# All 28 product tiles of a group added by VectorE, in a fused Strassen-type feed-forward loop on one core

## The chip, the core and the metric

The kernel runs on one core of one Trainium2 chip. TensorE (PE) multiplies, ScalarE (ACT), VectorE (DVE) and GpSimd (POOL) do the elementwise work, SyncE (SP) issues the transfers. The metric is the device time of one launch in microseconds (us). Before the change the median of three runs is 1248.9 us (1247.93 to 1248.97).

## The reference, cut to what matters

One layer of a hybrid encoder over 1088 kept rows (1024 of a prompt and 64 of a sample). The change touches only its second half, the feed-forward block:

```
f = square(relu(rmsnorm(h, norm_ffn_w) @ w_up)) @ w_down    # 1024 -> 4096 -> 1024, float32
h = h + f
y = rmsnorm(h)
```

## The kernel before, in words

A float32 product is made of three passes: each operand is split into a rounded high part (`_hi`, written by ScalarE with a Copy) and the rest (`_lo`, written by VectorE as source minus high part), and `passes` (L1419) issues high x high, high x low and low x high.

The 4096 hidden columns are worked through in 16 groups of 256. In each group TensorE first runs `up(g)`: two blocks of 128 hidden columns (a=0 and a=1), each in two halves of the inner dimension and three column ranges, 144 matmuls. ScalarE applies relu and square into `fr`. Then comes the down product. Groups 0 to 14 do it with seven products of 512x128x512 blocks in place of eight (a Strassen-Winograd scheme); the last group does it plainly. TensorE's order of products is P1, P2, P6, P5, P7, P4, P3. Each has four quarters q = 0 to 3 of three matmuls of 128x512, so 84 matmuls, and then `sample` adds 8 more. The operands of a product are one combination of `fr` blocks and one of `w_down` blocks:

```
P1: A11 x B11   P2: A12 x B21   P6: S2 x T2   P5: S1 x T1   P7: S3 x T3   P4: A22 x T4   P3: S4 x B22
```

S1 (sum) and S2 (difference) are built by VectorE (L1279, L1282), S3 and S4 by GpSimd, and T1, T3, T2, T4, in that order, by GpSimd from the loaded `w_down` blocks (L1386 to L1391). T4 is the last of a chain of dependent subtractions.

The products lie in eight PSUM banks: P1, P6, P7, P4 of a quarter share one bank (`BANK1`), P2, P5, P3 another (`BANK2`). P6, P7, P4 and P3 accumulate on what the bank holds, so between two products of a bank its content must have been taken: a quarter of P6 waits for the add of P1's same quarter, P5 for P2's, P7 for P6's, P4 for P7's, P3 for P5's. What is taken is added into `h` in SBUF. Before the change VectorE does this for 20 of the 28 quarter tiles (`add`, L1249). The 8 of P6 and P3 are copied by ScalarE from PSUM to one of four `tmp` tiles (`copy_out`, L796) and added to `h` by GpSimd (L1378); TensorE waits there for the copy (`act_copy`), not for the add.

The order on each engine is written out by hand in a function `group(g)` per engine, and each step waits for counting semaphores. Counters are read by position: `D_HI`, `D_LO`, `F_HI`, `F_LO` list in which order the high and low parts come, and a consumer waits for the position of its part. For P6 that is the low part of S2 (`f_ready`). The high part of `up`'s a=1 weights is written by ScalarE in `up_split(g, "up", 0)`, its low part by VectorE in `split_ffn(g, "up", 1, 0)`; TensorE's second block waits for that (`w_split`). SP's queue holds the loads only: four of `w_down` (`dr`) a group and four of `w_up` (`raw`).

Of the kernel before, what the change touches and what calls it, by code (L numbers as in the profile page):

```python
# [98 lines left out]
DVE_ADDS = [(P1, 0), (P1, 1), (P2, 0), (P1, 2), (P1, 3), (P2, 1), (P2, 2), (P2, 3), (P5, 0), (P5, 1), (P7, 0), (P7, 1),  # L99
            (P7, 2), (P7, 3), (P5, 2), (P5, 3), (P4, 3), (P4, 0), (P4, 1), (P4, 2)]  # L100
COPIES = [(P6, 0), (P6, 1), (P6, 2), (P6, 3), (P3, 0), (P3, 1), (P3, 2), (P3, 3)]
NPROD = 30
NDVE, NCOPY = len(DVE_ADDS), len(COPIES)
# [33 lines left out]
def build(nc, x_prompt, x_sample, state_conv, state_ret, meta_tokens, norm_mix_w, w_in, conv_w, ret_gn_w,  # L137
# [3 lines left out]
    with ctx:  # L141
# [45 lines left out]
        tmp2 = sb("tmp2", [P, 512], r_norm)  # L187
        tmp3 = sb("tmp3", [P, 512], r_norm + 2048)
# [114 lines left out]
        act_copy = sem("act_copy")  # L303
        pool_add = sem("pool_add")
# [67 lines left out]
        F_HI = ["f1", "A11", "S3", "A12", "f2", "A22", "S2", "S1", "f12", "S4"]  # L372
# [54 lines left out]
        def _(sp):  # L427
# [111 lines left out]
            sp.wait_ge(pool_add, NCOPY * G_LAST + 4)  # L539
# [15 lines left out]
        def _(act):  # L555
# [252 lines left out]
            def group(g):  # L808
                act.wait_ge(prod_done, NPROD * g + 1)
                up_split(g, "up", 0)  # L810
                d_hi(g, "B11")
                d_hi(g, "T1")
                d_hi(g, "B21")
                d_hi(g, "T3")
                act.wait_ge(f_ready, NF_PARTS * g + 1)
                relu(g, 0, 0)
                d_hi(g, "B22")
                square(g, 0, 0)
                relu(g, 0, 1)
# [20 lines left out]
                f_hi(g, "S1")  # L840
                copy_out(g, P6, 0)
                act.wait_ge(f_ready, NF_PARTS * g + F_LO.index("f1") + 2)
                act.activation(sf[:, 3, :], sf[:, 0, :].bitcast(F32), ACT.Copy, scale=-1.0).then_inc(neg_ready, 1)
                f_hi(g, "f12")
                copy_out(g, P6, 1)
                f_hi(g, "S4")
                copy_out(g, P6, 2)
                copy_out(g, P6, 3)
                copy_out(g, P3, 0)
                up_split(g, "next", 1)  # L850
                copy_out(g, P3, 1)
                copy_out(g, P3, 2)
                copy_out(g, P3, 3)
# [34 lines left out]
            def last_group(g):  # L888
# [3 lines left out]
                act.wait_ge(pool_add, NCOPY * g + 4)  # L892
# [36 lines left out]
        def _(dve):  # L929
# [27 lines left out]
            dve.sem_inc(pool_add, 4)  # L957
# [303 lines left out]
            def group(g):  # L1261
                split_ffn(g, "up", 1, 0)
                d_low(g, "B11", D_LO)
                split_ffn(g, "up", 1, 1)
                d_low(g, "T1", D_LO)
                d_low(g, "B21", D_LO)
                d_low(g, "B22", D_LO)
                f_low(g, "A11", F_HI)
                d_low(g, "T4", D_LO)
                f_low(g, "f1", F_HI)  # L1270
                split_ffn(g, "next", 0, 0)
                d_low(g, "T2", D_LO)
                f_low(g, "S3", F_HI)
                d_low(g, "T3", D_LO)
                f_low(g, "A12", F_HI)
                add(g, P1, 0)
                dve.wait_ge(fr_ready, 6 * g + 6)
                dve.tensor_tensor(f12[:, :], fr[:, 0, SEQ:TY], fr[:, 1, SEQ:TY], ALU.add).then_inc(f_sum_dve, 1)
                dve.tensor_tensor(fo_raw[:, P5, :], fr[:, 0, 512:1024], fr[:, 1, 512:1024], ALU.add).then_inc(f_sum_dve, 1)  # L1279
                dve.wait_ge(f_sum_dve, 3 * g + 2)  # L1280
                dve.wait_ge(f_sum_pool, 2 * g + 1)
                dve.tensor_tensor(fr[:, 0, 512:1024], fo_raw[:, P5, :], fr[:, 0, 0:512], ALU.subtract).then_inc(f_sum_dve, 1)  # L1282
                add(g, P1, 1)
                add(g, P2, 0)
                f_low(g, "S2", F_HI)
                add(g, P1, 2)
                add(g, P1, 3)
                f_low(g, "S1", F_HI)
                add(g, P2, 1)
                add(g, P2, 2)  # L1290
                add(g, P2, 3)
                add(g, P5, 0)
                f_low(g, "f2", F_HI)
                add(g, P5, 1)
                f_low(g, "A22", F_HI)
                add(g, P7, 0)
                add(g, P7, 1)
                add(g, P7, 2)
                add(g, P7, 3)
                f_low(g, "S4", F_HI)  # L1300
                add(g, P5, 2)
                add(g, P5, 3)
                f_low(g, "f12", F_HI)
                add(g, P4, 3)
                add(g, P4, 0)
                sample_add(g, 0)
                add(g, P4, 1)
                split_ffn(g, "next", 0, 1)
                add(g, P4, 2)
                sample_add(g, 1)  # L1310

# [60 lines left out]
        def _(pool):  # L1372
            def add(g, p, q):
                k = COPIES.index((p, q))
                pool.wait_ge(act_copy, NCOPY * g + k + 1)
                if p == P3:
                    pool.wait_ge(pool_add, NCOPY * g + n_copy(P6, q) + 4)
                pool.tensor_tensor(h_part(p, q), tmp(k), h_part(p, q), ALU.add).then_inc(pool_add, 1)  # L1378

            def group(g):  # L1380
# [14 lines left out]
                pool.wait_ge(f_sum_dve, 3 * g + 3)  # L1395
# [3 lines left out]
                add(g, P6, 2)  # L1399
                add(g, P6, 3)  # L1400
                add(g, P3, 0)
                add(g, P3, 1)
                add(g, P3, 2)
                add(g, P3, 3)
# [13 lines left out]
        def _(pe):  # L1418
# [212 lines left out]
            def up(g, first):  # L1631
                for a in range(2):
# [5 lines left out]
                    for half, j in order:  # L1638
# [24 lines left out]
            def product(g, p, q, first):  # L1663
# [19 lines left out]
                elif p == P7:  # L1683
                    pe.wait_ge(act_copy, NCOPY * g + n_copy(P6, q))
# [8 lines left out]
            def sample(g):  # L1693
# [74 lines left out]
```

## Time and profile before

| | before |
|---|---|
| median of 3 runs | 1248.9 us |
| the profiled execution's own time | 1246.07 us |
| its span | 1244.1 us |
| PE busy | 1226.6 us (99%), 6792 matmuls |
| DVE busy | 748.3 us (60%) |
| ACT busy | 500.5 us (40%) |
| POOL busy | 290.1 us (23%) |
| granted TensorE clock, mean | 0.997 |

The span is what the profile's clock covers; 1.97 us of the execution lie around it. A busy share is an average over the whole span. The feed-forward loop (groups 0 to 14) fills roughly the second half of it. A matmul's recorded duration overlaps with the next one's, so the pace is read from the difference of two starts.

### The profile page before, as it was taken

How to read it: one execution, taken by the hardware profiler on the slowest of the kernel's cores; microseconds unless marked ns; L12 is line 12 of the kernel's file. 1: busy time of each engine (PE TensorE's matmuls, PEld its weight loads, DVE VectorE, ACT ScalarE, POOL GpSimd, SP SyncE). 2: the span in 40 equal slices, each digit the busy share in tenths (PEclk: the TensorE clock that was granted, in tenths of full speed). 3: DMA queues.
4: the chain of work that ended last, by engine and by line, in shares of the span. 5: the costliest groups of instructions: out<-in, count | busy, mean ns of one | idle time of the engine just before them, and what ended most of it. 6: DMA issues, size and time to landing. Idle time of an engine off the chain costs nothing.

```text
span 1244.1 us, 20364 instructions
## 1 busy us (share of the span) xinstructions
PE 1226.6 (99%) x6792; PEld 1134.6 (91%) x6792; DVE 748.3 (60%) x1334; ACT 500.5 (40%) x1046; POOL 290.1 (23%) x221
## 2 busy tenths in 40 slices
PE   8999999999999999999999999999999999999997
PEld 5999999999999888889989989989988998998995
DVE  6555355355354554385686676677568667666747
ACT  6232232232232332255445335434544443543546
POOL 0000000000000000034533543352353354345212
PEclk9999999999999999999999999999999999999999
DMA  7111111111111530121012021021111202202103
GB/s 235 48 39 35 48 37 45 44 30 44 47 36 53 194 94 1 61 67 57 20 59 67 8 67 59 8 67 59 42 34 59 67 8 63 63 8 67 51 17 144
DMA packets 88353, 70.17 MB, mean 56 GB/s; under 512 B 9456, under 2 KB 73072, under 8 KB 88320
## 3 DMA queue, kind: packets, MB, share of 16 engines
q1 hardware_dynamic: 88320, 69.73, 18.3%
q8 instruction: 20, 0.33, 0.1%
q14 instruction: 13, 0.11, 0.0%
HBM read 64.73 MB, written 4.99 MB: 56 GB/s over the span
## 4 chain that ended last, share of the span: by engine, by line
PE 95%; DVE 2%; issue 1%; ACT 1%; DMA 1%; SPq 0%; POOLq 0%; POOL 0%; DVEq 0%; ACTq 0%
PE ps L1421 29%; PE ps L1423 29%; PE ps L1422 29%; PE ps L1427 1%; PE ps L1428 1%; PE ps L1599 1%; PE ps L1520 1%; PE ps L1538 1%; PE ps L1527 1%; PE ps L1537 1%; PE ps L1506 1%; PE ps L1438 0%; DMA raw<-in_w_up 0%; DVE hw L1338 0%; PE ps L1544 0%
## 5 line engine op out<-in xcount | busy, mean ns | idle before, releaser
L1421 PE MATMUL ps<-mid_hi,ws_hi 128*128 128x368 f32 (+1 forms) x768 | 251.3, 327 | 3.0 <-DVE ws_lo L1210 3.0
L1423 PE MATMUL ps<-mid_hi,ws_lo 128*128 128x368 f32 (+1 forms) x768 | 251.4, 327 | 0.0
L1422 PE MATMUL ps<-mid_lo,ws_hi 128*128 128x368 f32 (+1 forms) x768 | 250.7, 326 | 0.0
L1421 PE MATMUL ps<-hn_hi,ws_hi 128*128 128x368 f32 (+1 forms) x648 | 219.7, 339 | 1.2 <-DVE hn_lo L976 1.2
L1422 PE MATMUL ps<-hn_lo,ws_hi 128*128 128x368 f32 (+1 forms) x648 | 213.1, 329 | 0.0
L1423 PE MATMUL ps<-hn_hi,ws_lo 128*128 128x368 f32 (+1 forms) x648 | 213.0, 329 | 0.0
L1254 DVE TENSOR_TENSOR h<-ps,h 128x512 f32<-128x512 f32 x300 | 194.0, 679 | 9.1 <-PE ps L1423 9.1
L1378 POOL TENSOR_TENSOR h<-tmp,h 128x512 f32<-128x512 f32 x120 | 159.0, 1355 | 126.1 <-ACT tmp L799 126.1
L1421 PE MATMUL ps<-do_hi,fo_hi 128*128 128x512 f32 x452 | 176.3, 390 | 0.0
L1422 PE MATMUL ps<-do_lo,fo_hi 128*128 128x512 f32 x452 | 176.1, 390 | 0.0
L1423 PE MATMUL ps<-do_hi,fo_lo 128*128 128x512 f32 x452 | 176.0, 389 | 0.0
L1421 PEld LDWEIGHTS ps<-mid_hi,ws_hi 128*128 128x128 f32 x768 | 144.1, 188 | 4.2 <-DVE ws_lo L1210 3.3
L1210 DVE TENSOR_TENSOR ws_lo<-raw,ws_hi 128x512 fp32r<-128x512 f32 x64 | 60.5, 947 | 143.1 <-ACT ws_hi L753 143.1
L1422 PEld LDWEIGHTS ps<-mid_lo,ws_hi 128*128 128x128 f32 x768 | 144.2, 188 | 0.6
L1423 PEld LDWEIGHTS ps<-mid_hi,ws_lo 128*128 128x128 f32 x768 | 144.2, 188 | 0.0
L1386 POOL TENSOR_TENSOR do_raw<-dr 128x512 f32<-128x512 f32 x15 | 19.2, 1282 | 527.4 <-DMA dr<-in_w_down 526.8
L799 ACT ACTIVATE tmp<-ps 128x512 f32<-128x512 f32 x120 | 67.4, 597 | 151.1 <-PE ps L1423 151.1
L1421 PEld LDWEIGHTS ps<-hn_hi,ws_hi 128*128 128x128 f32 x648 | 121.8, 188 | 3.9 <-DVE hn_lo L976 2.4
L1422 PEld LDWEIGHTS ps<-hn_lo,ws_hi 128*128 128x128 f32 x648 | 121.9, 188 | 0.0
L1423 PEld LDWEIGHTS ps<-hn_hi,ws_lo 128*128 128x128 f32 x648 | 121.7, 188 | 0.0
L1421 PEld LDWEIGHTS ps<-do_hi,fo_hi 128*128 128x128 f32 x452 | 84.8, 188 | 18.5 <-DVE fo_lo L1247 0.3
L1423 PEld LDWEIGHTS ps<-do_hi,fo_lo 128*128 128x128 f32 x452 | 84.9, 188 | 18.0
(194 smaller groups left out, 1746.3 us busy)
## 6 DMA issues: line engine op xcount, KB each, us to landing
raw<-in_w_up SPq DMA_DIRECT2D x64, 256.0 KB, 4.8
dr<-in_w_down SPq DMA_DIRECT2D x64, 256.0 KB, 3.5
raw<-in_w_in SPq DMA_DIRECT2D x56, 256.0 KB, 2.9
raw<-in_w_out SPq DMA_DIRECT2D x16, 256.0 KB, 3.1
out<-hw SPq DMA_DIRECT2D x16, 256.0 KB, 2.1
xr<-in_x_prompt SPq DMA_DIRECT2D x7, 512.0 KB, 6.1
h<-in_x_prompt SPq DMA_DIRECT2D x2, 1024.0 KB, 10.8
h<-in_x_prompt SPq DMA_DIRECT2D x1, 2048.0 KB, 9.7
```

Of the source, the lines that this page charges most:

```text
L799: act.activation(tmp(k), bank_of(p, q)[:, :], ACT.Copy).then_inc(act_copy, 1)
L1210: dve.tensor_tensor(ws_lo[:, half], raw[:, s, :].rearrange("p (k c) -> p k c", k=4), ws_hi[:, half].bitcast(F32), ALU.subtract).then_inc(w ...
L1254: dve.tensor_tensor(h_part(p, q), bank_of(p, q)[:, :], h_part(p, q), ALU.add).then_inc(dve_add, 1)
L1378: pool.tensor_tensor(h_part(p, q), tmp(k), h_part(p, q), ALU.add).then_inc(pool_add, 1)
L1386: pool.tensor_tensor(t1, b12, b11, ALU.subtract).then_inc(d_sum, 1)
L1421: pe.matmul(out, a_hi, b_hi, start=start, stop=False, skip_group_check=again)
L1422: pe.matmul(out, a_hi, b_lo, start=False, stop=False, skip_group_check=again)
L1423: return pe.matmul(out, a_lo, b_hi, start=False, stop=stop, skip_group_check=again)
L1427: pe.matmul(out, a_hi_lo, b_hi, start=start, stop=False)
L1428: return pe.matmul(out, a_hi_lo, b_lo, start=False, stop=stop)
L1506: last = pe.transpose(out[:, c * P:(c + 1) * P], src[:, at:at + P], ident[:, :])
L1520: last = pe.matmul(out[:, c * HD:(c + 1) * HD], kd[:, c, :], v_tok[:, c0 + c, :], start=True, stop=True)
```

## The change

`COPIES`, the two semaphores and the four `tmp` steps of the middle go: no ScalarE copy out of PSUM and no GpSimd add in groups 0 to 14. VectorE's table has all 28 tiles, and every wait of TensorE on a copy becomes one on a VectorE add. The written orders of ScalarE and VectorE, and the four position lists, are new throughout.

```diff
-DVE_ADDS = [(P1, 0), (P1, 1), (P2, 0), (P1, 2), ... (P4, 1), (P4, 2)]
-COPIES = [(P6, 0), (P6, 1), (P6, 2), (P6, 3), (P3, 0), (P3, 1), (P3, 2), (P3, 3)]
+DVE_ADDS = [(P1, 0), (P1, 2), (P1, 1), (P1, 3), (P2, 0), (P2, 3), (P2, 2), (P6, 2), (P2, 1), (P6, 0), (P6, 1),
+            (P6, 3), (P7, 0), (P5, 1), (P7, 1), (P7, 3), (P7, 2), (P5, 0), ... (P3, 3), (P3, 1)]
-        F_LO = ["A11", "f1", "S3", "A12", "S2", "S1", "f2", "A22", "S4", "f12"]
+        F_LO = ["A11", "f1", "S3", "A12", "S1", "S2", "f2", "A22", "S4", "f12"]
-        D_HI = ["B11", "T1", "B21", "T3", "B22", "T2", "T4"]
-        D_LO = ["B11", "T1", "B21", "B22", "T4", "T2", "T3"]
+        D_HI = ["B11", "T4", "T3", "T1", "B22", "T2", "B21"]
+        D_LO = ["T4", "T3", "B22", "T2", "T1", "B11", "B21"]
...
             def group(g):                                   # ScalarE
                 act.wait_ge(prod_done, NPROD * g + 1)
+                d_hi(g, "B11")
+                d_hi(g, "T4")
+                d_hi(g, "T3")
                 up_split(g, "up", 0)
-                d_hi(g, "B11")
-                d_hi(g, "T1")
-                d_hi(g, "B21")
-                d_hi(g, "T3")
...
             def group(g):                                   # GpSimd
-                add(g, P6, 0)
-                add(g, P6, 1)
...
-                add(g, P3, 3)
...
                 elif p == P7:
-                    pe.wait_ge(act_copy, NCOPY * g + n_copy(P6, q))
+                    pe.wait_ge(dve_add, NDVE * g + n_dve_add(P6, q))
```

The negation of `f1` and the high part of the next group's second weight half also move forward on ScalarE, the small sum `f12` moves back on VectorE, and the load of the final norm weights no longer waits for GpSimd's adds, since the tiles that shared its place are gone.

Three places are shown as they stand in the engines' instruction orders. In the rows, `h<-ps` is an add of a tile, `fo_lo<-fr` the low part of A12 (first) or S2 (second), `fo_lo<-fo_raw` that of S1, `fo_raw<-fr` the sum S1, and `fr<-fo_raw,fr` the difference S2; ps0, ps1, ps2, ps6 are the banks of P1's quarters 0, 1, 2, 3.

VectorE at the first products of a group, before:

```order
L1254 TENSOR_TENSOR h_106<-ps0,h_106 128x512 [waits prod_done]
...
L1279 TENSOR_TENSOR fo_raw_55<-fr_61 128x512
...
L1282 TENSOR_TENSOR fr_61<-fo_raw_55,fr_61 128x512 [waits f_sum_pool]
...
L1254 TENSOR_TENSOR h_106<-ps1,h_106 128x512 [waits prod_done]
...
L1254 TENSOR_TENSOR h_106<-ps7,h_106 128x512 [waits dve_add]
...
L1247 TENSOR_TENSOR fo_lo_54<-fr_61,fo_hi_53 128x512 [waits f_hi_ready]
```

And the same place of the kernel after:

```order
L1229 TENSOR_TENSOR h_104<-ps0,h_104 128x512 [waits prod_done]
...
L1253 TENSOR_TENSOR fo_raw_55<-fr_61 128x512 [waits fr_ready]
...
L1229 TENSOR_TENSOR h_104<-ps2,h_104 128x512 [waits prod_done]
...
L1257 TENSOR_TENSOR fr_61<-fo_raw_55,fr_61 128x512 [waits f_sum_pool]
...
L1222 TENSOR_TENSOR fo_lo_54<-fo_raw_55,fo_hi_53 128x512 [waits f_hi_ready]
...
L1229 TENSOR_TENSOR h_104<-ps1,h_104 128x512 [waits prod_done]
...
L1229 TENSOR_TENSOR h_104<-ps6,h_104 128x512 [waits prod_done]
...
L1222 TENSOR_TENSOR fo_lo_54<-fr_61,fo_hi_53 128x512 [waits f_hi_ready]
```

The low part of S2 had two adds between it and the difference; it now has the low part of S1 and two adds, and one more add (P1's quarter 2) stands ahead of the difference.

VectorE a little later, after only: the adds of P2's quarters 3 and 2 (ps5, ps4), P6's quarter 2 (ps2), P2's quarter 1 (ps3) and P6's quarter 0 (ps0).

```order
L1229 TENSOR_TENSOR h_104<-ps5,h_104 128x512 [waits dve_add]
...
L1229 TENSOR_TENSOR h_104<-ps4,h_104 128x512 [waits dve_add]
L1225 REGISTER_ALU
L1229 TENSOR_TENSOR h_104<-ps2,h_104 128x512 [waits prod_done]
L1225 REGISTER_ALU
L1228 REGISTER_ALU [waits prod_done]
L1229 TENSOR_TENSOR h_104<-ps3,h_104 128x512 [waits dve_add]
L1225 REGISTER_ALU
L1229 TENSOR_TENSOR h_104<-ps0,h_104 128x512 [waits prod_done]
```

P2's quarter 1 is now taken behind P6's quarter 2; before, all of P2 was taken ahead of anything of P6.

ScalarE at a group's start, before, where `ws_hi` is the high part of the a=1 weights and `do_hi` that of a `w_down` block (from `dr`) or of a T (from `do_raw`):

```order
L753 ACTIVATE ws_hi_66<-raw_68 128x512 [waits raw_in0]
L771 REGISTER_ALU
L774 ACTIVATE do_hi_56<-dr_108 128x512 [waits dr_in0]
L773 ISA
L774 ACTIVATE do_hi_56<-do_raw_58 128x512 [waits d_sum]
```

And after:

```order
L764 ACTIVATE do_hi_56<-dr_106 128x512 [waits dr_in0]
L763 ISA
L764 ACTIVATE do_hi_56<-do_raw_58 128x512 [waits d_sum]
L763 REGISTER_ALU
L764 ACTIVATE do_hi_56<-do_raw_58 128x512 [waits d_sum]
L787 ISA
L742 REGISTER_ALU [waits w_used]
L743 ACTIVATE ws_hi_66<-raw_68 128x512 [waits raw_in0]
```

The high part of the weights stood first and now stands behind those of T4 and T3.

## Rows read from the trace of the kernel before

**Rows 1.** The page: busy share, and the costliest rows of lines (engine, shape, count | busy, mean ns | idle before)

```profile
PE 1226.6 (99%) x6792; PEld 1134.6 (91%) x6792; DVE 748.3 (60%) x1334; ACT 500.5 (40%) x1046; POOL 290.1 (23%) x221
...
L1421 PE MATMUL ps<-mid_hi,ws_hi 128*128 128x368 f32 (+1 forms) x768 | 251.3, 327 | 3.0 <-DVE ws_lo L1210 3.0
...
L1254 DVE TENSOR_TENSOR h<-ps,h 128x512 f32<-128x512 f32 x300 | 194.0, 679 | 9.1 <-PE ps L1423 9.1
L1378 POOL TENSOR_TENSOR h<-tmp,h 128x512 f32<-128x512 f32 x120 | 159.0, 1355 | 126.1 <-ACT tmp L799 126.1
```

**Rows 2.** Busy by stretch: stretch, us, PE, PEld, DVE, ACT, POOL, PEclk, DMA, GB/s

```profile
854.64:899.29 44.65, 44.65 (x238) 40.97 (x237) 30.40 (x46) 20.24 (x42) 18.67 (x14) 1.00 0.15 47
...
654.00:698.60 44.60, 44.60 (x238) 40.96 (x237) 30.41 (x47) 20.25 (x42) 18.66 (x15) 1.00 0.16 47
```

**Rows 3.** Timeline, PE, one group's first products: start, duration, what

```profile
899.29 0.40 PE L1421 MATMUL ps<-do_hi,fo_hi 128*128 128x512 f32 x1
...
899.76 0.39 PE L1423 MATMUL ps<-do_hi,fo_lo 128*128 128x512 f32 x1
...
901.12 0.39 PE L1423 MATMUL ps<-do_hi,fo_lo 128*128 128x512 f32 x1
...
904.75 0.39 PE L1421 MATMUL ps<-do_hi,fo_hi 128*128 128x512 f32 x1
```

**Rows 4.** Timeline, DVE, the same group

```profile
900.18 0.69 DVE L1254 TENSOR_TENSOR h<-ps,h 128x512 f32<-128x512 f32 x1 [0.18 <-PE ps L1423]
...
903.61 0.76 DVE L1247 TENSOR_TENSOR fo_lo<-fr,fo_hi 128x512 fp32r<-128x512 f32 x1
...
908.98 1.32 DVE L1243 TENSOR_TENSOR sf<-fr,sf 128x64 fp32r<-128x64 f32 x1
...
910.82 1.21 DVE L1247 TENSOR_TENSOR fo_lo<-fr,fo_hi 128x512 fp32r<-128x512 f32 x1
911.95 2.47 DVE L1254 TENSOR_TENSOR h<-ps,h 128x512 f32<-128x512 f32 x4
914.34 0.68 DVE L1247 TENSOR_TENSOR fo_lo<-fo_raw,fo_hi 128x512 fp32r<-128x512 f32 x1
```

**Rows 5.** Timeline, ACT, the same group

```profile
899.99 0.50 ACT L784 ACTIVATE fr<-fr 128x352 f32<-128x352 f32 x1
```

**Rows 6.** Timeline, POOL, the same group and the four T of the group's start

```profile
878.24 1.28 POOL L1386 TENSOR_TENSOR do_raw<-dr 128x512 f32<-128x512 f32 x1
...
882.10 1.29 POOL L1391 TENSOR_TENSOR do_raw<-dr,do_raw 128x512 f32<-128x512 f32 x1
...
902.51 1.30 POOL L1396 TENSOR_TENSOR fo_raw<-fr 128x512 f32<-128x512 f32 x1 [10.82 <-DVE fr L1282]
906.40 5.08 POOL L1378 TENSOR_TENSOR h<-tmp,h 128x512 f32<-128x512 f32 x4 [2.58 <-ACT tmp L799]
```

**Rows 7.** Timeline, group 0: PE, ACT, DVE and POOL

```profile
527.06 0.32 PE L1423 MATMUL ps<-mid_hi,ws_lo 128*128 128x352 f32 x1
530.37 0.43 PE L1421 MATMUL ps<-mid_hi,ws_hi 128*128 128x368 f32 x1 [2.98 <-DVE ws_lo L1210]
530.64 0.33 PE L1422 MATMUL ps<-mid_lo,ws_hi 128*128 128x368 f32 x1
...
528.50 0.61 ACT L774 ACTIVATE do_hi<-dr 128x512 fp32r<-128x512 f32 x1
529.02 0.61 ACT L774 ACTIVATE do_hi<-do_raw 128x512 fp32r<-128x512 f32 x1
...
528.62 1.69 DVE L1210 TENSOR_TENSOR ws_lo<-raw,ws_hi 128x512 fp32r<-128x512 f32 x1 [5.37 <-ACT ws_hi L753]
...
527.27 1.26 POOL L1386 TENSOR_TENSOR do_raw<-dr 128x512 f32<-128x512 f32 x1 [526.82 <-DMA dr<-in_w_down]
```

**Rows 8.** Busy by stretch, the span's start and group 0 (columns as in rows 2)

```profile
10.20:14.00 3.80, 3.80 (x10) 1.72 (x9) 3.73 (x6) 3.31 (x7) 0.00 (x0) 0.56 1.13 342
527.00:530.40 3.40, 0.41 (x4) 0.12 (x2) 1.78 (x2) 2.44 (x5) 3.13 (x3) 1.00 0.81 231
```

More of the change, by code:

```diff
@@ L835, in group @@
                 relu(g, 1, 2)
+                act.wait_ge(f_ready, NF_PARTS * g + F_LO.index("f1") + 2)
+                act.activation(sf[:, 3, :], sf[:, 0, :].bitcast(F32), ACT.Copy, scale=-1.0).then_inc(neg_ready, 1)
                 square(g, 1, 2)
+                up_split(g, "next", 1)
                 f_hi(g, "f2")
                 f_hi(g, "A22")
+                f_hi(g, "S1")
                 f_hi(g, "S2")
[L840 to L843, printed above, removed]
                 f_hi(g, "f12")
-                copy_out(g, P6, 1)
                 f_hi(g, "S4")
[L847 to L853, printed above, removed]
             with act.Fori(0, G_LAST) as g:
@@ L1261, in group @@
             def group(g):
+                d_low(g, "T4", D_LO)
                 split_ffn(g, "up", 1, 0)
-                d_low(g, "B11", D_LO)
+                d_low(g, "T3", D_LO)
                 split_ffn(g, "up", 1, 1)
-                d_low(g, "T1", D_LO)
-                d_low(g, "B21", D_LO)
+                f_low(g, "A11", F_HI)
+                f_low(g, "f1", F_HI)
                 d_low(g, "B22", D_LO)
[L1268 to L1271, printed above, removed]
                 d_low(g, "T2", D_LO)
                 f_low(g, "S3", F_HI)
-                d_low(g, "T3", D_LO)
+                d_low(g, "T1", D_LO)
+                d_low(g, "B11", D_LO)
+                d_low(g, "B21", D_LO)
+                split_ffn(g, "next", 0, 0)
                 f_low(g, "A12", F_HI)
@@ L1277, in group @@
                 dve.wait_ge(fr_ready, 6 * g + 6)
-                dve.tensor_tensor(f12[:, :], fr[:, 0, SEQ:TY], fr[:, 1, SEQ:TY], ALU.add).then_inc(f_sum_dve, 1)
                 dve.tensor_tensor(fo_raw[:, P5, :], fr[:, 0, 512:1024], fr[:, 1, 512:1024], ALU.add).then_inc(f_sum_dve, 1)
-                dve.wait_ge(f_sum_dve, 3 * g + 2)
+                add(g, P1, 2)
+                dve.wait_ge(f_sum_dve, 3 * g + 1)
                 dve.wait_ge(f_sum_pool, 2 * g + 1)
                 dve.tensor_tensor(fr[:, 0, 512:1024], fo_raw[:, P5, :], fr[:, 0, 0:512], ALU.subtract).then_inc(f_sum_dve, 1)
+                f_low(g, "S1", F_HI)
                 add(g, P1, 1)
+                add(g, P1, 3)
+                f_low(g, "S2", F_HI)
                 add(g, P2, 0)
[L1285 to L1288, printed above, removed]
+                f_low(g, "f2", F_HI)
+                add(g, P2, 3)
+                add(g, P2, 2)
+                add(g, P6, 2)
                 add(g, P2, 1)
-                add(g, P2, 2)
-                add(g, P2, 3)
-                add(g, P5, 0)
[L1293 to L1300, printed above, removed]
+                add(g, P6, 0)
+                f_low(g, "A22", F_HI)
+                add(g, P6, 1)
+                add(g, P6, 3)
+                dve.tensor_tensor(f12[:, :], fr[:, 0, SEQ:TY], fr[:, 1, SEQ:TY], ALU.add).then_inc(f_sum_dve, 1)
+                add(g, P7, 0)
+                add(g, P5, 1)
+                add(g, P7, 1)
+                add(g, P7, 3)
+                add(g, P7, 2)
+                f_low(g, "S4", F_HI)
+                add(g, P5, 0)
                 add(g, P5, 2)
                 add(g, P5, 3)
+                add(g, P3, 0)
                 f_low(g, "f12", F_HI)
@@ L1305, in group @@
                 add(g, P4, 0)
+                split_ffn(g, "next", 0, 1)
+                add(g, P3, 2)
+                add(g, P4, 1)
                 sample_add(g, 0)
-                add(g, P4, 1)
-                split_ffn(g, "next", 0, 1)
                 add(g, P4, 2)
+                add(g, P3, 3)
                 sample_add(g, 1)
+                add(g, P3, 1)
             with dve.Fori(0, G_LAST) as g:
@@ L1372, in _ @@
         def _(pool):
[L1373 to L1378, printed above, removed]
             def group(g):
```

56 lines of the change are left out of this document (19 added, 37 removed).

## The prediction, made before the changed kernel ran

> **What bounds the kernel now.** I read the page first: PE is busy 99% of the span, DVE 60%, ACT 40%, POOL 23% [rows 1]. Then the busy table by stretch, one group each: a group takes 44.60 to 44.65 us and PE is busy for all of it, at granted clock 1.00 [rows 2]. The list of waits has no PE wait inside groups 1 to 14. The only one of the feed-forward part is in group 0, 2.98 us, where PE waits for VectorE's low part of the second weights [rows 1, 7]. So PE sets the time, and nothing that ACT, DVE or POOL are spared can be won back, except 2.98 us in group 0 and what the pace of matmuls varies: the two stretches differ by 0.05, which over 15 groups is 0.75 us. The question is therefore not how much work goes, but whether every wait of PE still ends ahead of it under the new orders.
>
> **Whether VectorE has the capacity.** A group now has 8 more adds. Four adds in a row and the next start are 914.34 - 911.95 = 2.39 apart, so an add takes 0.60 of the queue, though it is recorded as 0.68 [rows 4]. That adds 8 x 0.60 = 4.8 us. Some comes back. The 64-column low part takes 1.32 us at 908.98 while POOL adds (906.40, four of 1.27 each), and the low part of A22 takes 1.21 in place of 0.68 [rows 4, 6]. Both have two operands in SBUF and wait for POOL's instruction to end; the PSUM adds beside them don't. Without POOL's adds some 1.1 + 0.5 = 1.6 us return. The Trainium skill says the same ("SBUF — State Buffer", section "Who interferes with whom": VectorE with two SBUF inputs and a GpSimd instruction that reads SBUF lock each other out for a whole instruction), and by that rule alone the change would be free, which is the first rival below. VectorE goes from 30.40 to about 30.4 + 4.8 - 1.6 = 33.6 of 44.65 [rows 2]. As a mean it has room. The 120 ScalarE copies and 120 GpSimd adds that go [rows 1] were hidden under PE: worth 0.
>
> **Term 1, the low part of S2 in each of 15 groups.** I walk VectorE's new queue beside PE of the profiled group. P1's first matmul starts at 899.29, P6's at 904.75, 24 matmuls later, so a matmul takes p = 0.2275 [rows 3]. From the third matmul of a quarter (899.76) to its add (900.18) are 0.42 [rows 3, 4].
> - add of P1 quarter 0: 900.18, as before.
> - sum S1: 900.78. The last square of `fr` ends at 900.49 [rows 5]; the negation, now ahead of it, makes that less than 0.1 later, still in time.
> - add of P1 quarter 2: its third matmul is at 901.12 [rows 3], so 901.54. This is a new wait.
> - difference S2: 902.14. It ends at 902.83.
> - low part of S1: 902.74. ScalarE's queue up to its high part is square, weights, f2, A22, S1, about 900.49 + 0.5 + 0.15 + 0.5 + 0.6 = 902.3, in time. The high part of S2 follows the difference and is there at 903.5.
> - adds of P1 quarters 1 and 3: 903.34 and 903.94.
> - low part of S2: 904.54, ends 0.69 later at 905.23. POOL's S4 (1.30 long [rows 6]) starts when the low part of S1 lets go, about 903.4, and can add up to 0.1.
>
> Before, that low part ran from 903.61 to 904.37 [rows 4], 0.38 ahead of PE at 904.75. Now PE is 0.48 early. What a restart costs is in group 0: DVE ends at 528.62 + 1.69 = 530.31, PE starts at 530.37 (0.06), and its first matmul is recorded as 0.43 against 0.33 of the next ones, since its weights weren't loaded ahead (0.10) [rows 7]. So this stall is 0.48 + 0.16 = 0.64 us. Bounds: 0 if the adds ran closer than 0.60 apart (four would have to save 0.12 each), 0.75 with POOL's lock.
>
> **Term 2, two waits that the new add order makes.** (a) P5 quarter 1 waits for the add of P2 quarter 1, which now stands behind that of P6 quarter 2. Counted from P6's first matmul, P6's quarter 2 issues its last at 8p = 1.82, its add starts at +0.42, P2's at +0.60 and ends at +0.69: 3.53. PE wants P5 quarter 1 at 15p = 3.41. Late by 0.12, with the restart 0.28. (b) P4 quarter 2 waits for the add of P7 quarter 2, which stands behind that of quarter 3. From P7's first matmul: 11p + 0.42 + 0.60 + 0.69 = 4.21 against 18p = 4.10, late by 0.11, with the restart 0.27. In both VectorE is free when the product ends, so they don't hang on its load. Each lies between 0.1 (the weights of the waiting matmul load in the shadow of the one before) and 0.3; near zero if the adds come 0.1 sooner. I take 0.23 each, 0.46 together. Everything else that waits for an add (P7 for P6, P3 for P5, both blocks of `up` for P4 and P3, `sample`) comes out 0.3 us or more ahead; closest is P3's first quarter, behind P5's add and the low part of S4.
>
> Terms 1 and 2 are 0.64 + 0.46 = 1.1 us a group, and 15 groups 16.5 us. PE has no slack in which to catch up.
>
> **Term 3, group 0.** ScalarE now does the high parts of B11, T4 and T3 ahead of that of the a=1 weights. In groups 1 to 14 this is hidden: POOL no longer ends its adds at 878.2 and starts the four T when the last product ends, and PE needs the weights 12 us into the group. In group 0 there is no such lead: the `w_down` blocks land at 527.27 (the releaser of POOL's first T), when PE has just finished the first block (527.06) [rows 7]. Undisturbed, the four T take 882.10 + 1.29 - 878.24 = 5.15 [rows 6], so T4 is there at 532.42. High part of T4 532.5; that of T3 0.52 later (529.02 - 528.50 [rows 7]), 533.0; the weights 533.5 to 534.2; VectorE's low part to 534.9; PE at about 534.95. Before, 530.37 [rows 7]. That is 4.6 us, once. Bounds: 4.0 (ScalarE's queue pitch less) and 5.8 (VectorE in between, as in POOL's slower chain).
>
> PE is then idle for 7.6 us, from the end of its last matmul (527.06 + 0.32) to 534.95. An idle of 2.98 left the clock at 1.00 [rows 8]. At the span's start, after waits of a few us with few matmuls, the rows show a stretch at 0.56 of full speed, that is at the 1.2 GHz level nearly throughout 3.8 us [rows 8]: at half pace it loses 0.44 x 3.8 = 1.7 us. I add that 1.7 once; bounds 0 and twice that. The Trainium skill ("TensorE: Matmul & The Clock Gate", section "What's actually happening") has the engine fall to half clock after idleness; the rows at the start agree, and no row here shows it after an idle as long as this one.
>
> **Terms at nothing.** The load of the final norm weights starts earlier than it did; its first user comes over 20 us later. The rest of the ScalarE and VectorE reordering hides behind `up`, where both are often idle. The last group's order is unchanged except for one wait that is over by then.
>
> **Sum.** 16.5 + 4.6 + 1.7 = 22.8 us over the profiled execution: 1246.07 + 22.8 = 1268.9. The median shown is 2.8 above that execution, so on its scale 1248.9 + 22.8 = 1271.7; I predict 1271. Low end: half of terms 1 and 2 (8.3) with 4.0 is 1261. High end: 15 x 1.4 + 5.8 + 3.4 = 30.2, so 1279.
>
> **Rivals.**
> - *The freed lock wins; not slower.* VectorE gets 1.6 us a group back [rows 4, 6], and every new order ends in time. Place: the low part of S2 at 904.54; it decides if the queue ahead of it is 0.5 us shorter, and T4 must come by 528. For it: POOL's adds and ScalarE's copies are gone and PE alone was the bound. Against: the time is returned later than the place (from 908.98 on), and ahead of S2 no row shows a lock to lift. Price: -0.75 at best, 1248. Chance 7% (faster by over 0.2% 3%, within it 4%; 0.2%, 2.5 us, is what a measurement of this kernel can tell from no change).
> - *Only group 0.* Terms 1 and 2 are too large by 0.5 and 0.1 us each, and PE's waits end in time; 4.6 + 1.7 remain: 1255. For it: the margins are below 0.5 us. Against: two of the three follow from fixed durations. Chance 9%.
> - *VectorE becomes the bound in the products.* From P1's first add on it has 28 + 2 adds, S1, S2, four low parts and one of weights, 37 x 0.60 = 22.2 us, beside 92 matmuls x 0.2275 = 20.9 of PE, and only the tail in `up` takes the rest. If an add beside busy PE costs its recorded 0.68, 28 x 0.08 = 2.2 more a group come on top less some 1 us of margin: 15 x 1.2 = 18, so 1289. Against: rows 4 show 0.60. Chance 9%.
> - *The forecast*, 1261 to 1279: 75%.
>
> The range that I give is 1257 to 1281. Faster 0.03, same 0.04, slower 0.93.
>
> **What would show it.** In the profile after: PE idle before lines of P6's first matmul, by the low part of S2, about 0.5 to 0.6 us in each of 15 groups; two more of 0.1 to 0.3 by VectorE's adds; in group 0 an idle of 7.6 in place of 2.98, by the low part of the weights, and after it a stretch at half clock; a group of 45.7 in place of 44.6; VectorE's 64-column low part back at 0.2. The forecast is wrong if a group stays at 44.7, if the waits of PE name something else (a copy of the weights, S4, `sample`), or if group 0 alone differs.

## The result, and the profile after

The changed kernel takes **1275.25 us** (median of four runs, 1272.81 to 1276.42), the kernel before 1248.66 in the same comparison (1247.93 to 1248.97). The ratio is 1.0214, with a 95% interval of 1.0201 to 1.0228. The change costs 26.6 us, 2.1%. The profiled execution of the changed kernel took 1272.81 us, its span is 1271.0. Against the profiled execution before (1246.07) that is 26.7 more, where the forecast had 22.8.

The page of the changed kernel: busy time by engine, and the rows of part 5 that answer to [rows 1].

```profile
PE 1240.2 (98%) x6792; PEld 1132.4 (89%) x6792; DVE 777.6 (61%) x1454; ACT 438.4 (34%) x926; POOL 131.7 (10%) x101
...
L1229 DVE TENSOR_TENSOR h<-ps,h 128x512 f32<-128x512 f32 x420 | 272.5, 685 | 25.5 <-PE ps L1391 21.6
L1389 PE MATMUL ps<-mid_hi,ws_hi 128*128 128x368 f32 (+1 forms) x768 | 252.4, 329 | 7.8 <-DVE ws_lo L1185 7.8
...
L1389 PE MATMUL ps<-do_hi,fo_hi 128*128 128x512 f32 x452 | 181.7, 402 | 8.9 <-DVE fo_lo L1222 8.3
```

ScalarE lost 62 us of work and GpSimd 158, VectorE gained 29, and PE, which does the same 6792 matmuls, now waits. The list of waits of PE gives the same two by line, time, count and longest:

```profile
PE ps L1389 <- DVE fo_lo L1222: 8.3, 15, 0.6
PE ps L1389 <- DVE ws_lo L1185: 7.8, 1, 7.8
```

Fifteen waits of 0.55 for the low part of S2, and one of 7.8 in group 0. These two sums understate the first: a start of PE can be late with no idle written beside it. So I read the starts. In full flow they are 0.2275 apart [rows 3]. Three places of each group stand out, here in the profiled group (PE, start and duration first):

```profile
875.24 0.39 PE L1391 MATMUL ps<-do_hi,fo_lo 128*128 128x512 f32 x1
876.18 0.49 PE L1389 MATMUL ps<-do_hi,fo_hi 128*128 128x512 f32 x1 [0.55 <-DVE fo_lo L1222]
876.51 0.39 PE L1390 MATMUL ps<-do_lo,fo_hi 128*128 128x512 f32 x1
...
879.49 0.39 PE L1391 MATMUL ps<-do_hi,fo_lo 128*128 128x512 f32 x1
879.90 0.50 PE L1389 MATMUL ps<-do_hi,fo_hi 128*128 128x512 f32 x1
...
885.95 0.39 PE L1391 MATMUL ps<-do_hi,fo_lo 128*128 128x512 f32 x1
886.36 0.50 PE L1389 MATMUL ps<-do_hi,fo_hi 128*128 128x512 f32 x1
...
922.28 0.49 PE L1389 MATMUL ps<-do_hi,fo_hi 128*128 128x512 f32 x1 [0.55 <-DVE fo_lo L1222]
```

- P6's first matmul (876.18) starts 0.94 after the one before it, and the next start is 0.33 later, since its weights weren't loaded ahead: 0.94 + 0.33 - 2 x 0.2275 = 0.82 us lost.
- P5's quarter 1 (879.90) and P4's quarter 2 (886.36): 0.41 and then 0.34 (the next starts are at 880.24 and 886.70), so 0.30 each. No idle is written beside them. That the weights come late here too stands in PE's weight loads: in full flow a load starts some 0.2 ahead of its matmul, here with it.
- The same place of the next group is at 922.28, 46.10 later, where a group took 44.65 [rows 2]. The three places make 1.42 of the 1.45.

```profile
879.90 0.19 PEld L1389 LDWEIGHTS ps<-do_hi,fo_hi 128*128 128x128 f32 x1 [0.44 <-DVE h L1229]
```

The busy table of this stretch (columns as in [rows 2]) has VectorE at 32.4, forecast 33.6, and a PE that is no longer busy throughout:

```profile
876.18:922.28 46.10, 45.51 (x237) 40.77 (x237) 32.44 (x55) 16.13 (x34) 8.17 (x6) 1.00 0.15 46
```

VectorE in that group, from P1's first add on. P1's first matmul is at 870.01, where [rows 3] have 899.29:

```profile
870.90 0.69 DVE L1229 TENSOR_TENSOR h<-ps,h 128x512 f32<-128x512 f32 x1 [0.18 <-PE ps L1391]
871.51 0.68 DVE L1253 TENSOR_TENSOR fo_raw<-fr 128x512 f32<-128x512 f32 x1
872.26 0.69 DVE L1229 TENSOR_TENSOR h<-ps,h 128x512 f32<-128x512 f32 x1
872.87 0.68 DVE L1257 TENSOR_TENSOR fr<-fo_raw,fr 128x512 f32<-128x512 f32 x1
873.47 0.69 DVE L1222 TENSOR_TENSOR fo_lo<-fo_raw,fo_hi 128x512 fp32r<-128x512 f32 x1
874.07 1.28 DVE L1229 TENSOR_TENSOR h<-ps,h 128x512 f32<-128x512 f32 x2
875.27 0.68 DVE L1222 TENSOR_TENSOR fo_lo<-fr,fo_hi 128x512 fp32r<-128x512 f32 x1
875.87 0.69 DVE L1229 TENSOR_TENSOR h<-ps,h 128x512 f32<-128x512 f32 x1
876.47 0.22 DVE L1218 TENSOR_TENSOR sf<-fr,sf 128x64 fp32r<-128x64 f32 x1
```

The low part of S2 starts 5.26 after P1's first matmul; the forecast's walk had 904.54 - 899.29 = 5.25. It ends at 875.95, and PE starts 0.23 later. The 64-column low part takes 0.22 in place of the 1.32 of [rows 4].

Group 0, timelines of ScalarE, VectorE and PE (against [rows 7]), then the busy table by stretch, with the clock after the column of POOL:

```profile
531.47 1.15 ACT L764 ACTIVATE do_hi<-do_raw 128x512 fp32r<-128x512 f32 x2 [8.27 <-POOL do_raw L1367]
532.52 0.61 ACT L743 ACTIVATE ws_hi<-raw 128x512 fp32r<-128x512 f32 x1
533.17 0.69 DVE L1185 TENSOR_TENSOR ws_lo<-raw,ws_hi 128x512 fp32r<-128x512 f32 x1 [0.35 <-ACT ws_hi L743]
533.91 0.68 PE L1389 MATMUL ps<-mid_hi,ws_hi 128*128 128x368 f32 x1 [7.84 <-DVE ws_lo L1185]
534.38 0.51 PE L1390 MATMUL ps<-mid_lo,ws_hi 128*128 128x368 f32 x1
```

```profile
527.20:533.90 6.70, 0.00 (x0) 0.00 (x0) 1.43 (x3) 2.44 (x6) 4.15 (x4) 0.74 0.14 39
533.90:540.00 6.10, 6.08 (x27) 6.09 (x28) 3.78 (x6) 4.24 (x10) 1.41 (x1) 0.72 0.00 0
540.00:547.00 7.00, 7.00 (x45) 7.00 (x44) 3.35 (x6) 3.91 (x8) 0.00 (x0) 1.00 0.04 14
```

PE is idle 7.84 in place of 2.98, and the clock falls during that idle. After it the matmuls start about 0.31 apart until 537.14 instead of 0.17. Forty steps from the restart on take 8.23 us, and 6.71 in the kernel before: 1.5 us. The other three runs of the changed kernel have a mean granted clock of 0.992 to 0.994 where the profiled one has 0.996, and are 1.5 to 3.6 us longer.

The account of the profiled execution goes by PE's starts. The first matmul of the down product is at 547.39 in group 0 and at 1238.87 in group 15, before at 542.33 and 1211.71: 691.5 us against 669.4, so 22.1 in the loop, or 1.47 a group. Group 0 adds 7.84 - 2.98 = 4.9 of idle and 1.5 of half clock. It loses 1.3 because the work ahead of the idle happened to run that much faster in this execution (PE's last matmul before it starts at 525.75 against 527.06 in [rows 7]). Together 27.2; the spans differ by 26.9, the times by 26.7.

### The profile page after: what moved, and what is told of

Its sections match the earlier page's. It is cut to its first block, busy times and chain, and to the rows that moved or that the text cites. A ratio compares the mean times of both kernels' runs of the same rounds, so it can differ in the third digit from the quotient of the medians.

```text
span 1271.0 us, 20003 instructions
## 1 busy us (share of the span) xinstructions
PE 1240.2 (98%) x6792; PEld 1132.4 (89%) x6792; DVE 777.6 (61%) x1454; ACT 438.4 (34%) x926; POOL 131.7 (10%) x101
## 4 chain that ended last, share of the span: by engine, by line
PE 90%; DVE 5%; issue 2%; DMA 1%; ACT 1%; DVEq 0%; POOL 0%; SPq 0%; POOLq 0%; ACTq 0%
PE ps L1389 28%; PE ps L1391 27%; PE ps L1390 27%; DVE fo_lo L1222 2%; PE ps L1396 1%; PE ps L1395 1%; DVE h L1229 1%; PE ps L1567 1%; PE ps L1488 1%; PE ps L1506 1%; PE ps L1495 1%; PE ps L1505 1%; PE ps L1474 1%; DMA xr<-in_x_prompt 0%; DVE hn_lo L951 0%
## 5 line engine op out<-in xcount | busy, mean ns | idle before, releaser
L1229 DVE TENSOR_TENSOR h<-ps,h 128x512 f32<-128x512 f32 x420 | 272.5, 685 | 25.5 <-PE ps L1391 21.6
L1389 PE MATMUL ps<-do_hi,fo_hi 128*128 128x512 f32 x452 | 181.7, 402 | 8.9 <-DVE fo_lo L1222 8.3
L1390 PEld LDWEIGHTS ps<-do_lo,fo_hi 128*128 128x128 f32 x452 | 85.0, 188 | 15.9
L925 DVE TENSOR_TENSOR ws_lo<-raw,ws_hi 128x512 fp32r<-128x512 f32 x54 | 37.1, 689 | 88.6 <-ACT ws_hi L555 88.1
L1185 DVE TENSOR_TENSOR ws_lo<-raw,ws_hi 128x512 fp32r<-128x512 f32 x64 | 44.0, 689 | 70.3 <-ACT ws_hi L743 70.3
```

Source lines behind the costliest of these rows:

```text
L925: dve.tensor_tensor(ws_lo[:, s], raw[:, s, :].rearrange("p (k c) -> p k c", k=4), ws_hi[:, s].bitcast(F32), ALU.subtract).then_inc(w_split, 1)
L1185: dve.tensor_tensor(ws_lo[:, half], raw[:, s, :].rearrange("p (k c) -> p k c", k=4), ws_hi[:, half].bitcast(F32), ALU.subtract).then_inc(w ...
L1229: dve.tensor_tensor(h_part(p, q), bank_of(p, q)[:, :], h_part(p, q), ALU.add).then_inc(dve_add, 1)
L1389: pe.matmul(out, a_hi, b_hi, start=start, stop=False, skip_group_check=again)
L1390: pe.matmul(out, a_hi, b_lo, start=False, stop=False, skip_group_check=again)
```

## The experiments

Theory: three orders cost the time, each at the place that the forecast names (S2's part behind the S1 and P1 adds; two pairs of adds turned round; the a=1 weights behind T4 and T3). Main rival: 28 adds are simply too many for VectorE beside the products, whatever their order. Ratios are to the kernel before, run beside each.

**The a=1 weights first.** The changed kernel with one order undone:

```
# ScalarE, VectorE, start of a group
+up_split(g, "up", 0)   /  +split_ffn(g, "up", 1, 0)
 d_hi B11, T4, T3       /   d_low T4
-up_split(g, "up", 0)   /  -split_ffn(g, "up", 1, 0)
```

> The changed kernel with one thing undone: at a group's start ScalarE and VectorE split the a=1 weights ahead of T4 and T3 again. Theory (term 3 of the prediction): T4's chain held these weights up in group 0 alone. PE's idle there falls from 7.84 to about 3 us (weights landing only), the stretch at half clock after it goes with it, and a group of the loop stays at 46.1 us: 4.9 + 1.5 to 3.5 us less, 1267 to 1269. Rival (the second half of the weights or B11 is late next, since VectorE now sits before T4 instead): the idle in group 0 only moves to a later wait of the same group, and less than 3 us are won.

Measured 1268.99 us, ratio 1.0164 (1.0147 to 1.0181). PE's wait in group 0:

```profile
530.95 0.44 PE L1389 MATMUL ps<-mid_hi,ws_hi 128*128 128x368 f32 x1 [3.33 <-DVE ws_lo L1185]
```

The idle falls from 7.84 to 3.33 and the loop keeps its period (P6's first matmul at 873.27 and 919.41, 46.14). So the order of the weights made these 4.5 us of idle; the median is 6.3 lower. The median is at the upper end of the theory's range, but a part of the theory missed, for the half clock did not go with the long idle: from 531.77 to 535.15 matmuls still start up to 0.31 apart, though the profiled kernel before shows no half clock after 2.98.

**S1 and S2 as before.** The orders of the two sums' parts as before the change, the adds of P1 in quarter order; the rest as changed.

```
-F_HI = [.., "S1", "S2", ..]   DVE_ADDS = [(P1,0),(P1,2),(P1,1),(P1,3),..
+F_HI = [.., "S2", "S1", ..]   DVE_ADDS = [(P1,0),(P1,1),(P1,2),(P1,3),..
-S1, P1.2, S2, low S1, P1.1, P1.3, low S2
+S1, S2, P1.1, P1.2, low S2, P1.3, low S1
```

> The changed kernel, with the sum S1, the difference S2 and its low part back at the places in VectorE's queue that they had before the change (no add of P1's quarter 2 ahead of the difference, low part of S2 ahead of that of S1). Theory A (the three waits of a group are separate prices): the 0.82 us at P6's first matmul go, 15 x 0.82 = 12.3 us less, 1263. Theory B (VectorE's queue between P1 and P5 is full, and a wait taken away ahead comes back behind): P6 starts 0.8 us earlier but P2's quarter 1 is added only about 0.5 us earlier, so the wait at P5's quarter 1 grows from 0.29 to about 0.6, and a group falls from 46.1 to 45.6: 7.5 us less, 1268.

Measured 1265.96 us, ratio 1.0137 (1.0120 to 1.0153). PE at P5's quarter 1 and VectorE ahead of it:

```profile
878.07 0.39 PE L1391 MATMUL ps<-do_hi,fo_lo 128*128 128x512 f32 x1
878.76 0.50 PE L1389 MATMUL ps<-do_hi,fo_hi 128*128 128x512 f32 x1 [0.30 <-DVE h L1229]
879.10 0.40 PE L1390 MATMUL ps<-do_lo,fo_hi 128*128 128x512 f32 x1
```

```profile
873.57 0.81 DVE L1222 TENSOR_TENSOR fo_lo<-fr,fo_hi 128x512 fp32r<-128x512 f32 x1
874.30 0.68 DVE L1229 TENSOR_TENSOR h<-ps,h 128x512 f32<-128x512 f32 x1
...
876.10 0.21 DVE L1218 TENSOR_TENSOR sf<-fr,sf 128x64 fp32r<-128x64 f32 x1
876.24 3.07 DVE L1229 TENSOR_TENSOR h<-ps,h 128x512 f32<-128x512 f32 x5
```

P6 no longer waits, but the wait at P5's quarter 1 grows from 0.30 to 0.69 + 0.34 - 0.455 = 0.58. A group is 45.50 (878.76 to 924.26): of 0.82 only 0.60 came back. From 874.30 to the end of the five adds VectorE's starts stand 0.60 apart (0.13 behind the small one) without a pause. PE's wait at P6 had given this queue time, and without it the queue is late at the next place. The terms are not separable, as theory B had it; the measured median lies between the two theories.

**The turned adds put in order.** P2.1 ahead of P6.2, and P7.2 ahead of P7.3:

```
-P2.0, P2.3, P2.2, P6.2, P2.1   ..   P7.1, P7.3, P7.2
+P2.0, P2.3, P2.2, P2.1, P6.2   ..   P7.1, P7.2, P7.3
```

> The changed kernel with two swaps in VectorE's order: the add of P2's quarter 1 ahead of that of P6's quarter 2, and that of P7's quarter 2 ahead of that of quarter 3. Theory (term 2): both small waits come from an add queued behind one whose product has only just ended; they go whole, 0.59 us a group, 15 x 0.59 = 8.9 less, 1266, and PE's first matmul of P6 still waits 0.55 with a restart of 0.23 + 0.10. Rival (VectorE is simply full, so that the order of adds doesn't matter): the waits turn up at other quarters and a group stays above 45.9, within 3 us of 1275.

Measured 1265.41 us, ratio 1.0137 (1.0120 to 1.0154). Both small waits are gone, P6's stays, and a group is 45.46 (873.99 to 919.45). Taken off: 9.8 us of the median, 0.64 a group in the trace.

**Which wait stands first in PE's queue.** PE starts P6 0.23 after the low part's end. Behind the wait for that part its queue holds two more, for `d` and for the bank. Here the late one comes last:

```
-wait f_ready; wait d_ready; wait dve_add
+wait dve_add; wait d_ready; wait f_ready
```

> The changed kernel with nothing moved but the order of PE's own waits ahead of a product's first quarter: f_ready (the operand's low part) is waited for last, behind d_ready and dve_add. In the trace PE starts 0.23 us after the low part of S2 ends, but 0.05 us after an add that it waits for at a later quarter. Theory C (the waits behind the late one are still to be processed by PE's sequencer once it is released): the start falls to 0.05 to 0.1 us behind, 0.13 to 0.18 a group, 2 to 2.7 us less in all, 1272.5 to 1273. Rival (the 0.23 belongs to the low part as a written operand, or to its weights' load): no change, a group stays at 46.1.

Measured 1273.04 us, ratio 1.0192 (1.0175 to 1.0209).

```profile
877.76 0.39 PE L1391 MATMUL ps<-do_hi,fo_lo 128*128 128x512 f32 x1
878.53 0.50 PE L1389 MATMUL ps<-do_hi,fo_hi 128*128 128x512 f32 x1 [0.38 <-DVE fo_lo L1222]
```

```profile
877.80 0.68 DVE L1222 TENSOR_TENSOR fo_lo<-fr,fo_hi 128x512 fp32r<-128x512 f32 x1
```

PE now starts 0.05 after the part ends (878.48), as it does after an add, and the gap is 0.77 in place of 0.94. A group is 45.93 (878.53 to 924.46), 0.17 less. So the waits that stand behind a late one in the queue cost 0.17 to 0.18 us each time, although they are over. The trace shows this, the times alone don't: the median is 2.2 lower, as the theory had it, but the two intervals of the ratio overlap.

**All three orders mended, and the loop's two alone.** The first has the three edits above (the weights, S1 and S2, the turned adds), with all adds of P2 and P6 in quarter order and P5's quarter 0 taken ahead of P7's. The second leaves the a=1 weights behind T4 and T3.

> All 28 adds stay on VectorE, and all three causes are undone together: the weights' split first at a group's start, S1 and S2 in VectorE's queue as before the change, and the adds of P1, P2, P6 and P7 in the order of their quarters (P5's quarter 0 ahead of P7's). Theory (the loss is order alone, VectorE has room for 28 adds): no wait of PE in groups 1 to 14, a group of 44.6 to 44.7 us, an idle of about 3.3 in group 0, and 1248 to 1250, that is the time of the kernel before, within 1.5 us. Rival (VectorE is the bound of the products, so that some wait stays whatever the order): a group of 45.0 or more, 1254 or more.

> As the kernel with all three undone, but the weights of group 0 still stand behind T4 and T3. Theory: the loop is free of waits (44.6 to 44.7 a group) and what is left is group 0 alone: 4.9 us of idle more and 1.5 to 3.5 us of half clock behind it, 1254 to 1257. Rival (the idle in group 0 pushes the products of group 0 or later ones out of step, or the loop gives nothing back without it): over 1259.

Measured 1250.77 (ratio 1.0022, 1.0013 to 1.0030) and 1255.10 (1.0049, 1.0035 to 1.0062). 24 of the 26.6 us are gone, so the orders made them, though the first stays 0.8 above its theory's range. In both a group is 44.83 (871.89 to 916.72 in the first), 0.18 over [rows 2], one wait at P4's quarter 1. The first kernel's VectorE there:

```profile
869.70 0.21 DVE L1273 TENSOR_TENSOR f<-fr 128x64 f32<-128x64 f32 x1
869.83 3.20 DVE L1229 TENSOR_TENSOR h<-ps,h 128x512 f32<-128x512 f32 x5
```

Five adds take 3.20 here, 3.07 in the run of S1 and S2 above. P5.1 and P7.1 stand side by side here and add into the same part of `h`, so the kernel makes the second wait by a semaphore for the end of the first. It starts 0.72 after it (870.43 and 871.15), where others start 0.60 apart. The second kernel, idle 8.39 in group 0, differs from the first by 4.3 us.

**All three, and the loads of `w_up` first.** In group 0 `w_down`'s blocks are asked for ahead of `w_up`'s. The edit, on the kernel with all three orders mended and on the kernel before itself:

```
-load_down(0, True)
 group(0, False)
+load_down(0, True)
```

> The kernel with all three undone, and in SP's queue the four w_up loads of group 0 ahead of its four w_down loads, which wait for the last transposition. Theory: the only wait left in the feed-forward part is for the landing of these weights; they come earlier, the idle of about 3 us goes and with it any stretch at half clock, 1245 to 1246, faster than both kernels by 3 us. Rival (the splits of these weights wait for PE to be done with the first block anyway, so the earlier landing is hidden): under 1 us less than without it.

> The kernel before the change with only the swap of loads in group 0. Theory (where the adds are done is worth nothing once nothing waits for them; only the load order is worth 3 us): the same 1245 as the kernel with 28 VectorE adds and this swap, within 1 us. Rival (VectorE freed from waiting on GpSimd's adds is worth something in the end): 1 us or more above that kernel.

Measured 1248.97 (ratio 1.0005, 0.9997 to 1.0014) and 1243.57 (0.9958, 0.9946 to 0.9971). Both theories missed: the first kernel won under 2 us by the swap, and the two are 5.4 apart where they were to be the same. PE's wait in the second block of `up` of group 0, first in the kernel with all three, then in the kernel before with swapped loads:

```profile
535.72 0.44 PE L1389 MATMUL ps<-mid_hi,ws_hi 128*128 128x368 f32 x1 [2.35 <-DVE ws_lo L1185]
...
536.16 0.47 PE L1391 MATMUL ps<-mid_hi,ws_lo 128*128 128x368 f32 x1
536.43 0.51 PE L1389 MATMUL ps<-mid_hi,ws_hi 128*128 128x368 f32 x1
```

```profile
534.74 0.43 PE L1421 MATMUL ps<-mid_hi,ws_hi 128*128 128x368 f32 x1 [0.98 <-DVE ws_lo L1210]
```

With the swap the wait moves from the first half of the a=1 weights to the second. What holds it for 2.35 in the first kernel is ScalarE, which still has T4 and T3 ahead of it (the row of two):

```profile
532.14 1.15 ACT L764 ACTIVATE do_hi<-do_raw 128x512 fp32r<-128x512 f32 x2 [5.33 <-POOL do_raw L1367]
...
534.32 0.62 ACT L743 ACTIVATE ws_hi<-raw 128x512 fp32r<-128x512 f32 x1
```

The kernel before won 4.6 us by the swap. Its two traces show 2.0 of that, 0.98 of idle for 2.98. The other runs with the loads as they were have a mean granted clock of 0.993 to 0.997, those with the swap 0.997 to 0.998, which fits a stretch at half clock in most of the former; no trace of one was kept.

**28 adds with every order as before.** This separates the route of the adds from the orders: no copies, no adds on GpSimd, but the parts of `d` and of the weights too in the order of the kernel before, and P5.1 ahead of P7.0. Once with the loads as they were, once swapped.

```
 D_HI, D_LO, F_HI, F_LO and both queues up to P1.0: as in the kernel before
-P5.0, P7.0, P5.1, P7.1     (of the kernel with all three mended)
+P5.0, P5.1, P7.0, P7.1
```

> All 28 adds on VectorE from PSUM and no copies, as in the changed kernel, but every order as in the kernel before: the d parts and the weight splits on ScalarE and VectorE, S2 ahead of S1, the adds in quarter order, and P5 q1's add two places behind P5 q0 and ahead of P7 q0's, so that no two adds into the same part of h stand side by side. Theory (the 28 adds cost nothing by themselves, only the orders did; the 0.18 us left per group with all three orders mended was the dependent pair of adds): group 44.65, no start of PE beyond 0.30 us in the loop, group 0 as before with 2.98 of idle; time 1247 to 1249, the same as before. Rival 1 (the eight further adds leave VectorE too full somewhere whatever the order): a wait of 0.2 to 0.6 us per group stays, group 44.8 to 45.3, time 1250.5 to 1258. Rival 2 (the GpSimd adds held VectorE up and their absence helps): below 1247.

> The same kernel, and the loads of w_up for group 0 issued ahead of those of w_down. If the two changes are independent it takes off what the load swap took off the kernel before, 4.6 us: 1243 to 1244.5 beside 1243.6 for the kernel before with the swapped loads, no half-clock stretch in group 0, and one wait of about 1 us for the second half of the a=1 weights. If the half-clock stretch after a 2.35 us idle comes back as in the run with all three mended and the loads swapped: 1246 to 1248.

Measured 1249.36 (ratio 1.0014, 1.0005 to 1.0023) and 1245.82 (0.9988, 0.9979 to 0.9997). The theory gave 1247 to 1249 and 1243 to 1244.5, so both missed, by 0.4 and 1.3 us. The rival of a wait whatever the order comes nearest. A group is 44.77, 0.12 over [rows 2], nearly the same in both. In the first kernel's group 0 the idle was 3.66, not 2.98, and a stretch at half clock followed (starts 0.31 apart from 532.30 to 535.36 in its trace), which the theory did not have either. The first kernel's VectorE and then PE:

```profile
870.42 0.21 DVE L1273 TENSOR_TENSOR f<-fr 128x64 f32<-128x64 f32 x1
870.55 3.07 DVE L1229 TENSOR_TENSOR h<-ps,h 128x512 f32<-128x512 f32 x5
```

```profile
871.88 0.50 PE L1389 MATMUL ps<-do_hi,fo_hi 128*128 128x512 f32 x1
872.22 0.39 PE L1390 MATMUL ps<-do_lo,fo_hi 128*128 128x512 f32 x1
```

P7.0 is the second of the five: 871.15 to 871.83, and P4's first matmul starts 0.05 later. Here the rival has a small part of the truth: the queue is full at this place, and a sum of 64 columns that nobody needs yet, at 870.42, takes 0.13 of it.

**That sum one place behind P7.0.** The last kernel, loads swapped:

```
-add P5.0; f12; add P5.1; add P7.0; add P7.1
+add P5.0; add P5.1; add P7.0; f12; add P7.1
```

> The kernel with the old orders and the loads swapped, with the 64-column sum f12 on VectorE one place behind P7 q0's add instead of two places ahead of it. In the run without this edit the queue is full from 864.36 on, f12 takes 0.13 us of it, and PE starts P4's first matmul at 867.62, 0.04 us after P7 q0's add ends, with 0.12 us lost per group (group 44.77). Theory (what is left of the change's cost is just this place of a full queue): the add ends 0.13 us earlier, the wait goes, group 44.65 to 44.68, 1.5 to 1.9 us in 15 groups: 1243.5 to 1244.8. Rival (the wait moves behind, to P4 q1 and P7 q1's add, as the other mended waits did): group 44.75 to 44.80, time 1245 to 1246.5.

Measured **1244.61** us (1243.68 to 1244.97), ratio 0.9973 (0.9963 to 0.9982). The time is in the theory's range, the group just above it: 44.70 (the second matmul of P4's quarter 1 at 823.24 and 867.94), with that matmul still 0.05 late. From group 0 to group 15 the first matmuls of the down product are 670.6 us apart (540.32 and 1210.95), in the kernel before with the same loads 669.5 (540.78 and 1210.31). So with the adds all from PSUM and the orders right, the change still costs 0.07 a group. The kernel beats both kernels by the loads, not by the change: the kernel before with the same loads stands at 0.9958.

## Why the prediction was right, and where it was off

The time, the sign and the three places came out as forecast (1271 against 1275.25). The sizes were too small together: in the profiled execution 22.1 + 4.9 + 1.5 = 28.5, forecast 22.8. That the total there is only 26.7 owes 1.3 us to luck, the faster work ahead of group 0. By its steps:

- **VectorE's walk** was exact: 5.25 forecast, 5.26 measured, each step 0.60 apart as read from [rows 4], so the rival in which adds cost their recorded 0.68 was wrong. The queue went to 32.4 of 46.1, not to the bound.
- **Term 1**, 0.64 a group forecast, 0.82 measured. The lateness was right; the restart was 0.16 from [rows 7], measured 0.23 + 0.10. In group 0 the waiting matmul has no further waits behind the late one, at P6 it has two. Reversing their order gave the 0.17 back.
- **Term 2**, 0.46 forecast, 0.59 measured. Its working gave 0.28 and 0.27, each measured 0.30. The step that failed is the choice of 0.23, taken because weights might load in the shadow. They don't: the load starts with the matmul (879.90), and the next start comes 0.34 later, as at the other wait. Putting the adds in order removed both.
- **Term 3**, 4.6 forecast, 4.9 measured; weights first took the idle to 3.33. The half clock came, 1.5 in the profiled execution against 1.7, and by the other runs' clocks more than that in them. This is the likely reason why the median is 2.4 above the profiled execution; the traces with S1 and S2 as before and with the order of PE's waits show such a longer stretch, to 542.10 and 542.23.
- **Terms at nothing**: the copies and the GpSimd adds were worth nothing. The last three kernels without them never beat the kernel with them, at equal loads.
- **The freed lock** returned what it should (0.22 for 1.32), behind the place that was late. The Trainium skill ("SBUF — State Buffer", section "Who interferes with whom") says that a VectorE instruction with two SBUF inputs contends with a GpSimd one that reads SBUF, and one with at most one SBUF input, outside the two-port modes, doesn't. The trace agrees: with S1 and S2 as before the low part of S2 beside GpSimd's sum S4 (872.53 to 873.83) takes 0.81 in place of 0.68, and the PSUM adds keep 0.60. That lock comes from S4 and not from the adds that went, so ahead of the place that was late the change gave nothing back.
- **Not in the forecast**: the terms can't be taken off one by one. The S2 order alone was worth 0.60 of its 0.82 a group, because the queue behind it was full. The forecast's own sum of 37 x 0.60 = 22.2 against 20.9 said this, and I used it only for a rival.

What stays open is the size of a rest of 1 to 2 us between the kernel with 28 adds and the kernel before, both with swapped loads. The medians differ by 1.0; the traces show 1.1 in the loop and 0.18 of wait in group 0 (1.16 against 0.98). The ratios, each against its own runs of the kernel before, differ by 0.0015, which is 1.9 us, with intervals of 0.0010 and 0.0013 to each side.

## What to carry to other kernels

Where one engine is busy all the time, work taken from the others is worth nothing, and every instruction that a reordering puts ahead of something that this engine needs can cost. Walk the feeding queue from the last fixed event with the pitch of its starts, not with recorded durations, and check each consumer's time against it, one by one. Mend all the late places together, because a wait that goes uncovers the next, and put the wait that comes last at the end of the list.

## What the runs showed of the hardware

- **A start after a wait.** PE starts 0.05 after its releaser ends when no wait stands behind the late one (878.48 to 878.53), 0.23 when two do (875.95 to 876.18). The weights of that matmul add 0.10 to 0.11 at each of these waits.
- **Dependent adds.** Two adds on VectorE of which the second waits by a semaphore for the end of the first start 0.72 apart (870.43 and 871.15), others 0.60.
- **The clock after short idles.** An idle of 2.98 [rows 7] left the clock at 1.00 in the profiled execution, and so did 0.98, 1.14 and 1.16 with the loads swapped. After 2.35, 3.33, 3.35 and 3.66 it fell to the 1.2 GHz level for some 3 us, the first longer step beginning 0.4 to 1.0 us after the restart. In the five runs with idles of 7.84 to 8.65 it fell during the idle. Two of them by stretch, first the kernel with weights first, then that with all three and swapped loads (idle 2.35; this stretch begins 1.3 us after the restart):

```profile
530.40:537.00 6.60, 6.05 (x27) 6.05 (x28) 2.48 (x4) 3.58 (x8) 2.91 (x2) 0.74 0.01 2
```

```profile
537.00:544.00 7.00, 7.00 (x35) 6.89 (x35) 6.36 (x10) 5.95 (x14) 1.40 (x1) 0.81 0.02 2
```

What in the 2.35 case brings the fall and in the 2.98 case doesn't, the runs don't tell. The price, forty steps from the restart on against the same forty at 1.00, was 1.4 to 1.6 us, and 2.6 to 2.7 in the two traces where the stretch lasted to 542.10 and 542.23: as much as the last terms of the loop.
